# A Hymba layer on one core: sample-step work moved to later attention tiles, and the first instructions of three stages moved ahead of the stage boundaries

## The chip, the cores and the metric

One core of one Trainium2 chip runs the whole kernel. The metric is the device time of one execution in microseconds, the median of three runs. TensorE's clock has two levels here, 1.2 and 2.4 GHz; the profile shows the granted clock as a share of the higher one.

## The reference

The kernel computes one layer of a hybrid decoder for 4096 prompt positions (and 16 meta tokens ahead of them) and for 8 x 8 sample-step tokens:

```python
z = rmsnorm(x, norm_w) @ w_in            # 1024 -> q 512 | k 128 | v 128 | g_attn 512 | u 512 | g_ssm 512
q, k = rope(rmsnorm(q)), rope(rmsnorm(k))
o = sink_softmax(q k / 8, window of 128, sinks) v       # 8 query heads, 2 kv heads
y, state = complex diagonal scan of u in 32 groups of 16 channels, 64 states each
a = rmsnorm(o * silu(g_attn), attn_out_norm_w)
g = gelu(y);  s = g * sigmoid(g @ w_glu + b_glu)
s = rmsnorm(s * silu(g_ssm), ssm_out_norm_w)
out = x + concat(a, s) @ w_out
```

The sample-step tokens attend to a cache of 128 keys and start from given states. Keys, values and states of both kinds of tokens are outputs too. Everything is float32; each product is made as three products of high and low parts (fp32r).

## The kernel before, in words

Four stages follow one another. Each is a block of five instruction streams (SP, POOL, PE, ACT, DVE), and between two blocks all five engines meet at a barrier. So nothing of a later stage starts before the last instruction, and the last awaited transfer, of the earlier one.

**Attention** (`attention_tiles`, names `b_`, PSUM `ps_b`) goes over NT = 33 tiles of 128 tokens. In a tile TensorE projects q, k, v and the gate, transposes keys (L1032, once per tile) and gates (L1038), makes the scores (L949) and the product with the values (L1016). The vector engine (DVE) masks the scores, splits the probabilities into high and low (`split_probs`, L1349), normalizes q and k (`norm_qk`, ends with `b_RK`), and multiplies the output by the gate (`gate_attn`, `b_AT`, L1387). POOL makes the low part of x (`b_XL`, L870), ACT the high part, copies and exponentials. The 64 sample-step tokens are a part of tile 0's projection, and their attention is done in pieces: `samples(t)` does one piece in tile t, at the tiles in `QK_AT, SCORES_AT, MAX_AT, ...`: 7 is the row maximum (DVE), 8 the exponentials (ACT), 9 the normalization (DVE), 10 to 15 the products, gate and norm. DVE's pieces stand between the rotation and `split_probs`; ACT's right after the tile's exponentials. The weights and x of the next stage are loaded, scaled and split here as well (`shared.load`, `shared.high` on ACT, `shared.low` on DVE, L391; `next_high_x` on ACT, `next_low_x` on POOL).

**Early projections** (`early_projections`, `e_`, `ps_e`) make u and the state-space gate in ST = 9 steps s of 464 tokens, each NB = 8 blocks m of 24 matmuls (L559 to L561): u for m = 0 to 3, the gate for m = 4 to 7. A block writes one of seven PSUM banks, and waits for the DVE to have emptied the block seven before (`z_out`). The last bank holds the sums of squares of x, by two matmuls with ones (`total(s)`, L546), from which DVE computes the norm (`rsqrt`, L88 to L94). In a step DVE does `u_out(s,0)`, a part of the state-space parameters (`discretize`), `u_out(s,1)`, `u_out(s,2)`, `discretize`, `u_out(s,3)`, then the gate blocks (`gate_in` L603, `gate_out` L608). SP stores u (L449) and the gate (L454, 36 transfers) to scratch, and at the end the second half of the parameters (`scr_par`, L177).

**State space** (`state_space`, `g_`, `ps_g`) goes over 32 groups. POOL makes tables (`phasors`), DVE small products (`vectors`, names `g_WB`, `g_CB`, `g_CP`), TensorE the group's matrices (L1612 to L1619) and its chunks (L1632); DVE turns inputs and scans. PARs (parameters) and U are loaded by SP from scratch.

**Late projections** (`late_projections`, `l_`, `ps_l`) in NJ = 9 blocks j of 512 tokens: `glu(j)` (48 matmuls, L2051 to L2053) on gelu's high and low parts (`l_GH` ACT, `l_GL` DVE), then per tile the output projection of the attention half (`attention_part(t,h)`, 12 matmuls, L2066 to L2068) and of the state half. SP loads A (attention output), Y, X and the gate in the order in which the code stands.

The order of the work around each boundary is that of the code, written out by hand; no planner moves anything.

Of the kernel before, what the change touches and what calls it, by code (L numbers as in the profile page):

```python
# [12 lines left out]
P = 128  # L13
# [17 lines left out]
T = 16  # L31
# [305 lines left out]
class Shared:  # L337
# [4 lines left out]
    def __init__(self, ctx, nc):  # L342
# [9 lines left out]
        self.XT = sb("XT", [P, KD, SW])  # L352
# [41 lines left out]

def early_projections(nc, I, scr, shared, RAO, USA):

# [4 lines left out]
    with ExitStack() as ctx:  # L401
# [8 lines left out]
        XH, XL = ([X0[hl], sb(f"X{hl}1", [P, KD, SW], F32R)] for hl in "HL")  # L410
# [24 lines left out]
        with nc.Block() as block:  # L435
            @block.sync
            def _(sp):
# [35 lines left out]
                par.store(sp, scr, 1)  # L473
# [8 lines left out]
            def _(act):  # L482
# [18 lines left out]
                for k in range(shared.STAGED, KD):  # L501
                    shared.high(act, k)
# [14 lines left out]
            def _(pool):  # L517
# [56 lines left out]
            def _(dve):  # L574
# [36 lines left out]
                for k in range(shared.STAGED, KD):  # L611
# [24 lines left out]
                for s in range(ST):  # L636
# [8 lines left out]
                    u_out(s, 3)  # L645
                    gate_in(s, 0)
# [21 lines left out]
def attention_tiles(nc, I, O, scr, shared):  # L668


    with ExitStack() as ctx:
# [93 lines left out]
        QK_AT, SCORES_AT, MAX_AT, EXP_AT, NORM_AT, CACHED_AT, NEW_AT, GATE_AT, VALUES_AT, SQUARE_AT, TOTAL_AT = 4, (5, 6), 7, 8, 9, 10, 11, 12, 13, 14, 15  # L765
# [9 lines left out]
        with nc.Block() as block:  # L775
            @block.sync
            def _(sp):
# [73 lines left out]
                for k in range(shared.STAGED, KD):  # L851
                    shared.load(sp, I, k)
                sp.wait_ge(gated, last)
                sp.dma_start(scr["a"][last * P:(last + 1) * P, :], AT[last % 2][:].rearrange("p c q -> p (c q)")).then_inc(a_st[last % 2], 16)
                sp.wait_ge(tail, 64)
# [5 lines left out]
            def _(pool):  # L861
# [43 lines left out]
                for p in range(3):  # L905
# [171 lines left out]
            def _(act):  # L1077
# [137 lines left out]
                for t in range(NT):  # L1215
                    if t >= 2:
                        square_a(t - 1)
                    if t == NT - 1:
# [3 lines left out]
                        shared.high(act, 1)  # L1222
                    if t:
                        exps(t)
                        samples(t)
# [19 lines left out]
                next_high_x(1)  # L1245
                shared.high(act, 2)
                shared.high(act, 3)
                next_high_x(2)
                shared.high(act, 4)
                next_high_x(3)  # L1250
# [4 lines left out]
            def _(dve):  # L1255
# [95 lines left out]
                def samples(t):  # L1351
# [8 lines left out]
                    elif t == MAX_AT:  # L1360
# [15 lines left out]
                    elif t == VALUES_AT:  # L1376
# [920 lines left out]
```

## Time and profile before

| what | value |
|---|---|
| time, median of 3 runs | 1875.1 us (1874.62 to 1875.12) |
| time of the profiled execution | 1875.93 us |
| its span, first to last instruction | 1874.1 us |
| TensorE busy | 1759.9 us, 94% |
| DVE, ACT, POOL busy | 72%, 36%, 28% |
| mean granted TensorE clock | 0.970 |

The times inside the profile are microseconds from the first instruction. 1.8 us of the execution lie around the span. Attention runs to about 750 us, the early projections to 1147, state space to 1388, late projections to the end. A matmul's row gives its start and its duration; matmuls overlap, so their durations do not add up to the time that they take.

### The profile page before, as it was taken

How to read it: one execution, taken by the hardware profiler on the slowest of the kernel's cores; microseconds unless marked ns; L12 is line 12 of the kernel's file. 1: busy time of each engine (PE TensorE's matmuls, PEld its weight loads, DVE VectorE, ACT ScalarE, POOL GpSimd, SP SyncE). 2: the span in 40 equal slices, each digit the busy share in tenths (PEclk: the TensorE clock that was granted, in tenths of full speed). 3: DMA queues.
4: the chain of work that ended last, by engine and by line, in shares of the span. 5: the costliest groups of instructions: out<-in, count | busy, mean ns of one | idle time of the engine just before them, and what ended most of it. 6: DMA issues, size and time to landing. Idle time of an engine off the chain costs nothing. (4 is left out here: it accounts for less than half of the span.)

```text
span 1874.1 us, 26223 instructions
## 1 busy us (share of the span) xinstructions
PE 1759.9 (94%) x8822; PEld 1428.2 (76%) x8822; DVE 1341.9 (72%) x2969; ACT 666.1 (36%) x1668; POOL 527.0 (28%) x618
## 2 busy tenths in 40 slices
PE   6899899999999996899999995999978999999999
PEld 4777677778777774788888883777756888888886
DVE  5787878687887887688989954898827545665632
ACT  5454444445445545332133201354424222222210
POOL 1122112121221222422223304899912101112110
PEclk8999999999999997899999997999988999999999
DMA  6211112142122101333143124566565553554331
GB/s 251 82 60 66 54 60 89 36 142 101 60 73 76 37 25 54 81 96 130 55 123 132 52 82 127 134 174 158 141 132 129 129 142 124 146 124 122 110 115 65
DMA packets 198406, 191.62 MB, mean 102 GB/s; under 512 B 121345, under 2 KB 157185, under 8 KB 198273
## 3 DMA queue, kind: packets, MB, share of 16 engines
q1 hardware_dynamic: 189056, 181.56, 32.9%
q10 hardware_dynamic: 9216, 8.39, 2.2%
q8 instruction: 71, 1.16, 0.3%
q14 instruction: 63, 0.51, 0.1%
HBM read 130.81 MB, written 59.10 MB: 101 GB/s over the span
## 5 line engine op out<-in xcount | busy, mean ns | idle before, releaser
L916 PE MATMUL ps_b<-b_WH,b_XH 128*128 128x512 f32 (+1 forms) x792 | 293.5, 371 | 17.5 <-DVE b_WL L1259 10.6
L917 PE MATMUL ps_b<-b_WL,b_XH 128*128 128x512 f32 (+1 forms) x792 | 283.6, 358 | 0.0
L918 PE MATMUL ps_b<-b_WH,b_XL 128*128 128x512 f32 (+1 forms) x792 | 283.6, 358 | 0.0
L916 PEld LDWEIGHTS ps_b<-b_WH,b_XH 128*128 128x128 f32 x792 | 151.7, 192 | 47.4 <-issue 26.0
L870 POOL TENSOR_TENSOR b_XL<-b_XT,b_XH 128x1024 fp32r<-128x1024 f32 x33 | 79.7, 2416 | 374.3 <-ACT b_XH L1088 324.4
L918 PEld LDWEIGHTS ps_b<-b_WH,b_XL 128*128 128x128 f32 x792 | 151.5, 191 | 22.2
L917 PEld LDWEIGHTS ps_b<-b_WL,b_XH 128*128 128x128 f32 x792 | 152.2, 192 | 19.2
L1154 ACT ACTIVATE b_SM<-ps_b,b_small 128x128 f32<-128x128 f32 x256 | 113.7, 454 | 109.9 <-DVE b_small L1330 107.3
L559 PE MATMUL ps_e<-w_X0H,w_nextH 128*128 128x464 f32 x320 | 123.7, 386 | 2.5 <-POOL e_ONES L518 2.5
L2066 PE MATMUL ps_l<-W_OUTH,l_AH 128*128 128x512 f32 (+1 forms) x264 | 106.7, 404 | 17.8 <-POOL l_AL L2015 13.1
L561 PE MATMUL ps_e<-w_X0H,w_nextL 128*128 128x464 f32 x320 | 121.2, 379 | 0.0
L2166 DVE SCALAR_TENSOR_TENSOR l_OUT<-ps_l,l_small,l_OUT 128x512 f32<-128x512 f32 (+1 forms) x66 | 48.8, 749 | 100.8 <-PE ps_l L2068 100.8
L560 PE MATMUL ps_e<-w_X0L,w_nextH 128*128 128x464 f32 x320 | 121.0, 378 | 0.0
L2015 POOL TENSOR_TENSOR l_AL<-l_A,l_AH 128x512 fp32r<-128x512 f32 (+1 forms) x33 | 42.4, 1286 | 237.9 <-ACT l_AH L1962 237.9
L2067 PE MATMUL ps_l<-W_OUTL,l_AH 128*128 128x512 f32 (+1 forms) x264 | 105.2, 398 | 0.0
L2068 PE MATMUL ps_l<-W_OUTH,l_AL 128*128 128x512 f32 (+1 forms) x264 | 105.0, 398 | 0.0
L2066 PE MATMUL ps_l<-W_OUTH,l_SH 128*128 128x512 f32 (+1 forms) x264 | 102.9, 390 | 0.0
L2068 PE MATMUL ps_l<-W_OUTH,l_SL 128*128 128x512 f32 (+1 forms) x264 | 102.8, 389 | 0.0
L2067 PE MATMUL ps_l<-W_OUTL,l_SH 128*128 128x512 f32 (+1 forms) x264 | 102.7, 389 | 0.0
L1962 ACT ACTIVATE l_AH<-l_A 128x512 fp32r<-128x512 f32 (+1 forms) x33 | 20.5, 622 | 228.9 <-DMA l_A<-scr_a 228.9
L498 ACT ACTIVATE e_TH<-e_TG 128x464 f32<-128x464 f32 x36 | 20.8, 592 | 224.8 <-DVE e_TG L603 224.8
L2158 DVE SCALAR_TENSOR_TENSOR l_OUT<-ps_l,RAO,l_X 128x512 f32<-128x512 f32 (+1 forms) x66 | 48.4, 748 | 72.8 <-DMA out_out<-l_OUT 51.3
(324 smaller groups left out, 4366.0 us busy)
## 6 DMA issues: line engine op xcount, KB each, us to landing
b_XT<-in_xb SPq DMA_DIRECT2D x33, 512.0 KB, 4.0
b_XR<-in_x SPq DMA_DIRECT2D x33, 512.0 KB, 4.7
w_XT<-in_xt SPq DMA_DIRECT2D x36, 464.0 KB, 3.6
l_X<-in_xr SPq DMA_DIRECT2D x32, 512.0 KB, 4.6
out_out<-l_OUT SPq DMA_DIRECT2D x32, 512.0 KB, 3.0
scr_gs<-e_TG SPq DMA_DIRECT2D x36, 232.0 KB, 2.0
scr_u<-w_ST SPq DMA_DIRECT2D x12, 696.0 KB, 3.8
g_U<-scr_u SPq DMA_DIRECT2D x192, 43.5 KB
```

What stands on the lines that cost most here:

```text
L559: pe.matmul(bank(s, m), high, XH[s % 2][:, k, :], start=(k == 0), stop=False)
L560: pe.matmul(bank(s, m), high, XL[s % 2][:, k, :], start=False, stop=False)
L561: mm = pe.matmul(bank(s, m), low, XH[s % 2][:, k, :], start=False, stop=(k == KD - 1))
L870: pool.tensor_tensor(XL[b][:], XT[b][:], XH[b][:].bitcast(F32), ALU.subtract).then_inc(x_lo, 1)
L916: pe.matmul(bank[:, 0:c1 - c0], XH[b][:, k, :], WH[:, k, c0:c1], start=(k == 0), stop=False)
L917: pe.matmul(bank[:, 0:c1 - c0], XH[b][:, k, :], WL[:, k, c0:c1], start=False, stop=False)
L918: mm = pe.matmul(bank[:, 0:c1 - c0], XL[b][:, k, :], WH[:, k, c0:c1], start=False, stop=(k == KD - 1))
L1154: exped.mark(act.activation(SM[:, h, :], scores_of(g)[:, j, t % 2, :], ACT.Exp, bias=NM[:, h:h + 1], scale=RQX[:, h:h + 1], accum_out=SUM[ ...
L2066: pe.matmul(bank, lh, w[0], start=first, stop=False)
L2067: pe.matmul(bank, lh, w[1], start=False, stop=False)
L2068: return pe.matmul(bank, ll, w[0], start=False, stop=last)
L2166: dve.scalar_tensor_tensor(out=o, in0=ps[0:n, 3 + 2 * h, :], scalar=RSS[0:n, i:i + 1], in1=o, op0=ALU.mult, op1=ALU.add).then_inc(o_out, 1)
```

## The change

**Attention.** The sample pieces from the maximum on move one or two tiles later. On ACT the pieces stand behind `values(t + 1)` instead of right behind the tile's exponentials. The maximum and the normalization on DVE become `sample_softmax(t)`, behind `gate_attn(t)`. At the end of the stage DVE makes two instead of three `shared.low` ahead of the last `gate_attn`, and does one more piece of the next x in POOL's place; ACT's and SP's work for the weight rows 1, 4 and 7 moves later.

**Early projections.** The wait for the ones and `total(0)` stand behind block 2 of step 0 instead of behind block 0. In the last step, SP, POOL and DVE do what was the start of state space: five parameter loads, `SWAP`, the store of the parameters ahead of the last gate stores, u of groups 0 and 1, the tables of groups 0 to 3, the vectors of groups 0 to 2. The class `Groups` holds the buffers of that, in room that x of the steps before has left.

**State space to late projections.** The class `Ahead` holds the attention outputs A of the tiles 0 and 1, which are loaded and split within state space. Four of the last eight stores of `scr_ys` go to ACT's queue, and SP no longer waits for 17 stores at the end of state space, but ahead of the last load of Y. In the late projections SP's first loads are X(0) and Y(0), TensorE does both parts of tiles 0 and 1 ahead of `glu(0)`, and DVE adds the attention of tile 0 ahead of `low_g(0)`.

```diff
-        QK_AT, SCORES_AT, MAX_AT, EXP_AT, NORM_AT, CACHED_AT, NEW_AT, GATE_AT, VALUES_AT, SQUARE_AT, TOTAL_AT = 4, (5, 6), 7, 8, 9, 10, 11, 12, 13, 14, 15
+        QK_AT, SCORES_AT, MAX_AT, EXP_AT, NORM_AT, CACHED_AT, NEW_AT, GATE_AT, VALUES_AT, SQUARE_AT, TOTAL_AT = 4, (5, 6), 8, 9, 10, 12, 13, 14, 15, 16, 17
...
                     if t:
                         exps(t)
-                        samples(t)
                     if t + 1 < NT:
                         copy_q(t + 1)
...
                         values(t + 1)
+                    samples(t)
                     if t + 2 < NT:
                         high_x(t + 2)
...
                     if t == NT - 1:
-                        for k in range(3):
+                        for k in range(2):
                             shared.low(dve, k)
                     if t + 1 < NT:
                         norm_qk(t + 1)
                         gate_of(t + 1)
                     if t:
                         gate_attn(t)
+                    sample_softmax(t)
...
+                    if s == ST - 1:
+                        sp.wait_ge(x_acc, 7 * ST)
+                        for t in range(groups.RP - 1):
+                            groups.load_params(sp, t)
+                        sp.wait_ge(z_full, NB * (ST - 1))
+                        sp.dma_start(groups.SWAP[:], I["swap"]).then_inc(groups.const_ld, 16)
                     for m in range(4):
                         if s + 2 < ST:
                             load_x(s + 2, m)
                         store_u(s, m)
+                    if s == ST - 1:
+                        par.store(sp, scr, 1)
+                        sp.wait_ge(u_st[0], 16 * ST // 3)
+                        for t in range(2):
+                            groups.load_u(sp, t)
                     for m in range(4):
                         store_g(s, m)
...
-                par.store(sp, scr, 1)
                 sp.wait_ge(par.stored, 32)
...
+                pool.wait_ge(z_full, NB * (ST - 1))
+                for t in range(4):
+                    groups.phasors(pool, t)
...
-                pe.wait_ge(ones_set, 1)
                 for s in range(ST):
                     for m in range(NB):
                         project(s, m)
-                        if s == 0 and m == 0:
+                        if s == 0 and m == 2:
+                            pe.wait_ge(ones_set, 1)
                             total(0)
...
                     u_out(s, 3)
+                    if s == ST - 1:
+                        for t in range(3):
+                            groups.vectors(dve, t)
...
-                load_params(0)
-                load_params(1)
-                for dst, src in ((SWAP, I["swap"]), (NO, I["out_norm"])):
-                    sp.dma_start(dst[:], src).then_inc(const_ld, 16)
-                for t in range(2, RP - 1):
-                    load_params(t)
-                load_u(0)
-                load_u(1)
-                load_u(2)
+                sp.dma_start(NO[:], I["out_norm"]).then_inc(const_ld, 16)
+                groups.load_u(sp, 2)
...
+                    if t in (20, 21):
+                        ahead.load(sp, t - 20, P, t - 19)
...
-                sp.wait_ge(out_st, 16 * 17)
...
+                    if t in (28, 29):
+                        ahead.low(pool, t - 28, P)
...
+                    if t in (24, 25):
+                        ahead.high(act, t - 24, P)
+                y_out.wait(act, tile(G - 1))
+                for i in range(4, 8):
+                    act.dma_start(scr["ys"][256:512, 8 * i:8 * i + 8].rearrange("(g h) b -> h g b", h=SG), YSS[SG * i:SG * i + SG, 16:32, :]).then_inc(out_st, 16)
...
-                load_a(0)
+                load_x(0)
                 load_y(0)
-                load_x(0)
-                load_a(1)
...
-                for h in range(2):
-                    attention_part(0, h)
+                for t in range(2):
+                    for h in range(2):
+                        attention_part(t, h)
                 glu(0)
-                for h in range(2):
-                    attention_part(1, h)
...
+                add_attention(0)
                 low_g(0)
-                add_attention(0)
                 steps(0)
```

On DVE, the sample maximum (`b_s_small`) stands in tile 7 between the end of the rotation (`b_RQK`) and the split of the probabilities (`b_PC`, `b_PP`):

```order
L1289 TENSOR_TENSOR b_RQK<-b_RQK,b_ZS 128x128
L1362 TENSOR_REDUCE b_s_small<-w_ST 128x4
L1364 TENSOR_TENSOR b_s_small<-b_s_small 128x4
L1366 TENSOR_TENSOR b_s_small<-b_s_small 128x4
L1367 TENSOR_SCALAR b_s_small<-b_s_small 128x4
L1349 TENSOR_TENSOR b_PC<-ps_b,b_HALF 128x512
L1349 TENSOR_TENSOR b_PP<-ps_b,b_HALF 128x512
```

In the changed kernel it stands on the same engine in tile 8, at the tile's end, between the gated output (`b_AT`) and the mask on the next tile's scores:

```order
L1416 TENSOR_TENSOR b_RK<-b_RQK,b_small 128x128
L1425 SCALAR_TENSOR_TENSOR b_GATE<-b_TH,ps_b 128x512
L1504 TENSOR_TENSOR b_AT<-ps_b,b_GT 128x512
L1483 TENSOR_REDUCE b_s_small<-w_ST 128x4
L1485 TENSOR_TENSOR b_s_small<-b_s_small 128x4
L1487 TENSOR_TENSOR b_s_small<-b_s_small 128x4
L1488 TENSOR_SCALAR b_s_small<-b_s_small 128x4
L1438 COPY_PREDICATED ps_b<-b_TAKE,ps_b 128x4x128
```

The four instructions have left the place ahead of `b_PC`, and stand behind `b_RK` and `b_AT`. On SP's queue, the boundary from the early projections (the last gate stores `scr_gs`, the parameter store `scr_par`) to state space (the two branches are the barrier) reads before:

```order
L449 DMA scr_u<-w_ST 128x1392 x4
L454 DMA scr_gs<-e_TG_10301 128x464
L454 DMA scr_gs<-e_TG_10302 128x464
L454 DMA scr_gs<-e_TG_10301 128x464
L454 DMA scr_gs<-e_TG_10302 128x464
L177 DMA scr_par<-params 128x16x198
L435 UNCONDITIONAL_BRANCH
L1491 UNCONDITIONAL_BRANCH
L1500 DMA g_PAR<-scr_par 128x198 x2
L1534 DMA g_SWAP<-in_swap 128x384
L1534 DMA g_NO<-in_out_norm 128x8
L1500 DMA g_PAR<-scr_par 128x198 x3
```

and in the changed kernel, at the same place:

```order
L548 DMA scr_u<-w_ST 128x1392 x4
L177 DMA scr_par<-params 128x16x198
L454 DMA g_U_10300<-scr_u 128x1x87 x6
L454 DMA g_U_10301<-scr_u 128x1x87 x6
L553 DMA scr_gs<-e_TG_10325 128x464
L553 DMA scr_gs<-e_TG_10326 128x464
L553 DMA scr_gs<-e_TG_10325 128x464
L553 DMA scr_gs<-e_TG_10326 128x464
L534 UNCONDITIONAL_BRANCH
L1635 UNCONDITIONAL_BRANCH
L1656 DMA g_NO<-in_out_norm 128x8
L454 DMA g_U_10302<-scr_u 128x1x87 x6
```

The parameter store and two groups of `g_U` have come ahead of the last four gate stores, and `g_PAR` and `g_SWAP` ahead of all that is shown; behind the barrier only `g_NO` and the third group's u are left ahead of the weights.

## Rows read from the trace of the kernel before

**Rows 1.** Windows: busy us (instructions) per engine, then granted clock, DMA share, GB/s

```profile
804.40:1088.00 283.60, 282.52 (x1328) 248.73 (x1327) 252.63 (x568) 75.34 (x94) 70.00 (x49) 1.00 0.30 94
1088.00:1135.30 47.30, 47.29 (x225) 41.77 (x223) 17.16 (x25) 2.96 (x5) 0.00 (x0) 1.00 0.23 91
1168.00:1380.10 212.10, 209.07 (x1040) 163.63 (x1040) 173.72 (x236) 93.86 (x316) 178.12 (x250) 0.98 0.59 146
1445.30:1874.00 428.70, 424.58 (x1906) 349.71 (x1906) 220.77 (x337) 89.53 (x142) 65.08 (x51) 0.99 0.43 121
```

**Rows 2.** Timeline of PE, key transposes: tiles 7 to 9, and twelve tiles later on

```profile
184.99 0.27 PE L1032 MATMUL ps_b<-b_ID,b_RK 128*128 128x128 f32 x1
...
208.24 0.33 PE L1032 MATMUL ps_b<-b_ID,b_RK 128*128 128x128 f32 x1 [1.12 <-DVE b_RK L1301]
...
233.24 0.33 PE L1032 MATMUL ps_b<-b_ID,b_RK 128*128 128x128 f32 x1 [1.12 <-DVE b_RK L1301]
...
258.57 0.33 PE L1032 MATMUL ps_b<-b_ID,b_RK 128*128 128x128 f32 x1 [1.12 <-DVE b_RK L1301]
...
372.71 0.27 PE L1032 MATMUL ps_b<-b_ID,b_RK 128*128 128x128 f32 x1
...
620.51 0.27 PE L1032 MATMUL ps_b<-b_ID,b_RK 128*128 128x128 f32 x1
```

**Rows 3.** Timeline of DVE: a sample piece in tile 7, and a steady tile

```profile
199.38 2.27 DVE L1364 TENSOR_TENSOR b_s_small<-b_s_small 128x4 f32<-128x4 f32 x1
...
603.10 0.70 DVE L1323 COPY_PREDICATED ps_b<-b_TAKE,ps_b 128x512 f32<-128x512 int32 x1 [2.22 <-PE ps_b L949]
```

**Rows 4.** Timelines of PE and DVE at the end of attention

```profile
739.46 1.92 PE L1016 MATMUL ps_b<-b_PP,b_VS 128*64 128x512 f32 x4
...
743.05 0.68 DVE L1387 TENSOR_TENSOR b_AT<-ps_b,b_GT 128x512 f32<-128x512 f32 x1
...
750.99 0.76 PE L559 MATMUL ps_e<-w_X0H,w_nextH 128*128 128x464 f32 x1 [2.49 <-POOL e_ONES L518]
```

**Rows 5.** Timelines of PE and DVE, step 0 of the early projections

```profile
764.46 1.14 PE L546 MATMUL ps_e<-e_ACC,e_ONES 128*128 128x464 f32 x1 [5.41 <-POOL e_ACC L532]
...
766.48 0.64 DVE L88 TENSOR_SCALAR e_VX<-ps_e 128x464 f32<-128x464 f32 x1 [10.80 <-PE ps_e L546]
...
794.28 1.00 DVE L595 TENSOR_TENSOR w_ST<-ps_e,e_RXB 128x400 f32<-128x400 f32 x1
...
804.37 0.38 PE L559 MATMUL ps_e<-e_XH,w_nextH 128*128 128x464 f32 x1
```

**Rows 6.** Windows, the stretch at the half clock behind a short wait of PE in the late projections

```profile
1422.50:1425.90 3.40, 3.40 (x9) 2.40 (x8) 1.61 (x2) 0.42 (x1) 0.00 (x0) 0.52 1.00 180
```

**Rows 7.** Timelines and waits of SP and PE, early projections to state space; last, the DMA issues

```profile
1137.65 0.46 SPq L177 DMA_DIRECT2D scr_par<-params  x1
SPq L435 <- DMA scr_par<-params: 6.2, 1, 6.2
1147.26 0.80 SPq L1500 DMA_DIRECT2D g_PAR<-scr_par  x2
1151.91 1.01 PE L1612 MATMUL ps_g<-g_CP,g_PAR 128*16 128x256 f32 x2 [16.63 <-DVE g_CP L1778]
1161.25 1.13 PE L1632 MATMUL ps_g<-g_U,g_W 128*128 128x265 f32 x4 [1.19 <-DMA g_U<-scr_u]
scr_gs<-e_TG SPq DMA_DIRECT2D x36, 232.0 KB, 2.0
```

**Rows 8.** Timelines and waits of SP and PE, state space to late projections

```profile
1381.30 3.91 SPq L1523 DMA_DIRECT2D scr_ys<-g_YSS  x8
SPq L1560 <- DMA out_states<-g_XS: 1.3, 1, 1.3
1388.72 5.75 SPq L1898 DMA_DIRECT2D l_Y<-scr_y  x4
1421.28 0.47 PE L2051 MATMUL ps_l<-l_GH,W_GLUH 128*128 128x512 f32 x1 [2.59 <-DVE l_GL L2114]
```

More of the change, by code:

```diff
@@ L351, in __init__ @@
         self.X0 = {hl: self.at("X", KD * SW * "HL".index(hl), "w_X0" + hl, [P, KD, SW], F32R) for hl in "HL"}
-        self.XT = sb("XT", [P, KD, SW])
+        self.XT = high.enter_context(nc.sbuf_tensor("w_XT", [P, KD, SW], F32, side="right"))
         self.ST = sb("ST", [P, 9 * (QK + P)])
@@ L398, in early_projections @@
+def early_projections(nc, I, scr, shared, groups, RAO, USA):
     NB, NPC = 8, 4
@@ L500, in _ @@
                 act.sem_inc(x_hi, NPC)
-                for k in range(shared.STAGED, KD):
+                for k in range(4, KD):
                     shared.high(act, k)
@@ L610, in _ @@
                 dve.sem_inc(x_lo, NPC)
-                for k in range(shared.STAGED, KD):
+                for k in range(3, KD):
                     shared.low(dve, k)
@@ L850, in _ @@
                 sp.dma_start(O["v_win"], VS[last % 3][:]).then_inc(tail, 16)
-                for k in range(shared.STAGED, KD):
-                    shared.load(sp, I, k)
+                shared.load(sp, I, 5)
+                shared.load(sp, I, 6)
                 sp.wait_ge(gated, last)
                 sp.dma_start(scr["a"][last * P:(last + 1) * P, :], AT[last % 2][:].rearrange("p c q -> p (c q)")).then_inc(a_st[last % 2], 16)
+                shared.load(sp, I, 7)
                 sp.wait_ge(tail, 64)
@@ L904, in _ @@
                         tables(t + 2)
-                for p in range(3):
+                for p in range(2):
                     next_low_x(p)
@@ L1245, in _ @@
                 next_high_x(1)
+                shared.high(act, 1)
                 shared.high(act, 2)
+                next_high_x(2)
+                next_high_x(3)
                 shared.high(act, 3)
-                next_high_x(2)
-                shared.high(act, 4)
-                next_high_x(3)
                 square_a(NT - 1)
@@ L1473, in tile @@
+        out_st = ahead.rest_st
         def tile(t):
@@ L1800, in scan @@
                     z_steps.link(dve, T_, dve.tensor_tensor(CZ[t % RM][:, :, 0:n], bcast_mid(ZS[:], 2), CS[t % RC][:, :, 0:n], ALU.mult))
-                for t in range(3):
-                    vectors(t)
                 turn_inputs(0)
                 turn_inputs(1)
-                vectors(3)
+                groups.vectors(dve, 3)
                 scan(0)
@@ L1836, in late_projections @@
         X = [sb(f"X{i}", [P, D]) for i in range(3)]
-        A = [sb(f"A{i}", [P, 4, P]) for i in range(2)]
-        AH, AL = ([sb(f"A{hl}{i}", [P, 4, P], F32R) for i in range(2)] for hl in "HL")
+        AH, AL = ahead.AH, ahead.AL
         OUT = [sb(f"OUT{i}", [P, D]) for i in range(2)]
@@ L1845, in late_projections @@
         y_ld, gs_ld = [sem(f"y_ld{i}") for i in range(2)], sem("gs_ld")
-        x_ld, a_ld = [sem(f"x_ld{i}") for i in range(3)], [sem(f"a_ld{i}") for i in range(2)]
+        x_ld = [sem(f"x_ld{i}") for i in range(3)]
         g_hi, g_lo = sem("g_high"), sem("g_low")
-        a_hi, a_lo = sem("a_high"), sem("a_low")
+        a_lo = ahead.lo
         z_full, z_th = sem("z_full"), sem("z_tanh")
@@ L1913, in load_a @@
                 def load_a(t):
[L1914 to L1917 removed]
+                    sp.wait_ge(a_lo, t - 1)
+                    ahead.load(sp, t, rows(t)[1], block_of(t))
                 def store(t):
@@ L1957, in high_a @@
                 def high_a(t):
-                    act.wait_ge(a_ld[t % 2], 16 * (t // 2 + 1))
-                    if t >= 2:
-                        act.wait_ge(a_full, 2 * (t - 1))
-                    n = rows(t)[1]
-                    act.activation(AH[t % 2][:, :, 0:n], A[t % 2][:, :, 0:n], ACT.Copy).then_inc(a_hi, 1)
+                    act.wait_ge(a_full, 2 * (t - 1))
+                    ahead.high(act, t, rows(t)[1])
                 def tanh(j, m):
@@ L2036, in _ @@
                         if t + 2 < NT:
-                            low_a(t + 2)
+                            ahead.low(pool, t + 2, rows(t + 2)[1])
             @block.tensor
```

253 lines of the change are left out of this document (146 added, 107 removed).

## The prediction

> **What bounds the kernel now.** I read the granted clock and the span first, then the windows by stage, then TensorE's waits, then timelines around each. Inside the stages TensorE is the bound: it is busy for 282.52 of 283.60 us in steps 1 to 7 of the early projections, 209.07 of 212.10 us in state space, 424.58 of 428.70 us in the late projections behind 1445.3 [rows 1]. So an edit inside these stretches gains nothing by itself, and a microsecond saved ahead of them is kept to the end. What is left are five places where TensorE stands. One is attention's tiles 7 to 9: the key transposes are 23.25, 25.00 and 25.33 us apart, 73.58 together, while later ones are (620.51 - 372.71)/12 = 20.65 us apart [rows 2]; three of these are 61.95, an excess of 11.6 us. The others are the end of attention (7.9 us from the last gated output to the next stage's first matmul, 2.49 of them the last wait [rows 4]), step 0 of the early projections (5.41 [rows 5]), the start of state space (16.63 and 1.19 [rows 7]) and the start of the late projections (2.59 [rows 8] and what is ahead of it). At each restart the clock is at its lower level for a while; behind the wait of 2.59 us it was granted 0.52 over 3.40 us [rows 6], which is 1.6 us of lost work.
>
> **The change part by part.**
>
> *Tiles 7 to 9: 9.4 us.* The sample maximum, exponentials and normalization are in these tiles, and they stand ahead of the work that feeds TensorE: DVE's ahead of the split probabilities, ACT's ahead of its copies. Behind `gate_attn` DVE has an idle stretch of 2.22 us in a steady tile, until scores come [rows 3]. The two DVE pieces move into that idle stretch. Their bulk before was one instruction on 128x4 elements that took 2.27 us [rows 3]; without such a stall the pieces are under 2 us each, so the idle stretch covers them. If that cover were gone they would cost what they cost now, 2.6 and 4.7 us (the periods less 20.65). ACT's exponentials move behind `values(t + 1)`; now they delay ACT's high part of x for tile t + 2, and so POOL's low part, which then falls on DVE's normalization. I leave 2.2 us for that, the stall of 2.27 seen once. 11.6 - 2.2 = 9.4. Both ends: 6 (a stall in each of the three tiles, 11.6 - 3 x 2.0) and 11.6 (nothing left). The later pieces (six, each moved by one or two tiles) cost nothing new, their TensorE work is the same.
>
> *End of attention and step 0: 5.5 us.* The last `b_AT` starts at 743.05, but its matmuls end at 739.46 + 1.92 = 741.4 [rows 4]; DVE was making the third `shared.low`. With two, `b_AT` starts at about 741.4 to 741.8. From there to the first matmul of the early projections is 750.99 - 743.05 = 7.9 us (POOL's sums, norm, store, barrier), which follows along; the ones (2.49 us wait, mostly barrier) are no longer waited for there. First matmul at about 749.0, 2.0 earlier. Then block 0 takes 764.46 - 5.41 - 750.99 = 8.06 us (half clock), and `total(0)` stood 5.41 us behind it. Now blocks 1 and 2 stand between: a warm block of 24 matmuls is 283.60/1328 x 24 = 5.1 us [rows 1]. `total(0)` is at 749.0 + 8.06 + 10.2 = 767.2; the sums that it needs were ready at 764.4 and come no later, so it does not wait. DVE reads them about 1 us later, at 768.2. Now something is late next: DVE's chain from there (norm, the low parts of x, `u_out(0,0)`, `discretize`, `u_out(0,1)`) took from 766.48 to 795.3 [rows 5], 28.8 us, and ends at 797.0. Block 0 of step 1 needs the bank that `u_out(0,1)` empties. TensorE gets there at 767.6 + 5 x 5.1 + 0.4 = 793.4 and waits for 3.6 us; queued behind are all its later blocks, and nobody but DVE's later outputs waits for these. It restarts at 797.0 against 804.37 [rows 5], 7.4 us earlier, and pays 1.6 to 1.9 us of half clock like [rows 6]: 5.5. Ends: 3 (a slower DVE chain beside POOL) and 10.9 (no wait: 2.0, the 5.41, and 3.5 us of half clock behind it).
>
> *Early projections to state space: 8.1 us.* Before, the parameters are stored at 1137.65, SP waits 6.2 us for their landing, and the first instruction of state space is at 1147.26, 2.9 us behind that; TensorE starts at 1151.91 [rows 7]. Now the parameter store is ahead of the gate stores and lands under them; the last thing awaited is the last gate store, issued right ahead of 1137.65 with 2.0 us to landing [rows 7], so 1139.7, and state space begins at 1142.6. Parameters, tables and vectors are there; what TensorE's stream still waits for is `g_NO`, issued first behind the barrier: 0.4 us of issue and a landing like the 2.0 of [rows 7]. It starts at 1145.0, 6.9 earlier; the u of group 1 is loaded too, so the 1.19 us wait goes. What is moved into step 8 counts there: on SP five parameter loads, `SWAP`, the store and 12 loads of u ahead of the gate stores; on POOL 32 table instructions; on DVE nine, of which three take less than the 4.7 us from 1147.26 to 1151.91. What hides them is step 8's TensorE work, 47.29 of 47.30 us, beside which DVE is busy for 17.16 us and POOL for nothing [rows 1]: 30 us are free on DVE for at most 14. Without that cover the last gate store comes late: 19 issues of 0.43 us (0.46 for the store, 0.80 for two loads [rows 7]) are 8.2 us on SP, and up to 3 of them could remain at the end. Ends: 5 and 9.
>
> The Trainium skill ("DMA: Bandwidth & Descriptors", Latency and other measured facts) gives a fixed cost of about 2 us to each DMA, however small. By it the load of `g_NO` behind the barrier keeps a wait of that size, and the term cannot reach the 9.3 us that no wait at all would give (1142.6 against 1151.91). The trace agrees (2.0 us [rows 7]).
>
> *State space to late projections: 2.1 us.* SP issues four stores fewer, 4 x 3.91/8 = 1.95, and does not wait 1.3 us for the last [rows 8]: the stage begins 3.3 earlier. A(0) needs no load, so TensorE works at once on the attention parts and the wait for `l_AL` as such goes; but the end is set by Y(0), gelu and `l_GL`. Y(0) is issued behind X(0)'s 512 KB instead of A(0)'s 256 KB; at 5.75 us for four Y of 256 KB that is 0.4 to 1.4, I take 0.8. `glu(1)` (1421.28 [rows 8]) comes 2.5 earlier. Since attention(1) no longer fills the time ahead of it, TensorE's 2.59 us wait grows to about 8, and the half clock behind it lasts longer; 0.4 for that. Ends 0 and 4.
>
> Sum 9.4 + 5.5 + 8.1 + 2.1 = 25.1. The profiled execution is 1875.93 us, 0.8 above the median 1875.1 of the runs shown: 1850.8, and on the median's scale 1850.0.
>
> **The rivals.** A change under 0.2%, 3.75 us, is about what cannot be told from none.
>
> - *No new wait in step 1* (chance 0.13). If DVE's chain is 4 us shorter beside an emptier POOL, +3.6 + 1.6; with nothing left of the excess in tiles 7 to 9, +2.2: a gain of 32.5, 1842.6. For it: DVE's chain there runs beside POOL, and two engines that hold each other up could fall otherwise. Against: POOL's work there is the same, and stands at the same place of the chain.
> - *The stalls move with the pieces* (0.10). The 2.27 us on 128x4 elements [rows 3] is DVE held up by something. Nine tiles hold moved pieces; at four more stalls, 9.1 lost, 1859. The Trainium skill ("SBUF — State Buffer", Who interferes with whom) names the cause: DVE and GpSimd share a port pair that one instruction locks as a whole. By it a piece moved beside POOL's low part of x stalls anew. The row agrees with a stall of that kind.
> - *The boundaries give less* (0.20). The chains behind them are not shortened as I think: 7 from the tiles, 3 at step 0, 4 and 0 at the boundaries, 14: 1861.
> - *Nothing in sum* (0.04): the place where TensorE waited is only given back by DVE later, at every one of the five: 1872 to 1878.
> - *DVE becomes the bound of the early projections* (0.03), the other side. The wait of 3.6 us at step 1 comes again in each of the seven steps behind it, 7 x (3.6 + 1.6) = 36.4, more than 25.1: 1886. It decides from 3.6 us per step without catching up. Against: DVE is busy for 252.63 of 283.60 us [rows 1], so 3.9 us per step are free, and it catches up in one.
>
> **How the numbers follow.** The forecast itself has 0.50, with 1846 to 1855. The range 1843 to 1862 takes in the smaller gains and all but the end of the larger, and leaves out about 2 in 10. Faster 0.93, same 0.04, slower 0.03.
>
> **What would show it.** In the profile after: key transposes 21 to 23 us apart all through tiles 7 to 10; the last `b_AT` at its matmuls' end; no wait at `total(0)`, one of 3 to 4 us on `u_out(0,1)` at step 1; the first matmul of state space 7 us earlier against step 8's end, waiting for `g_NO`; PE's first late matmul right behind the barrier, then a wait of about 8 us ahead of `glu(1)`. The prediction is wrong if step 8 has waits of TensorE, if tiles 8 to 17 show new long periods, or if the new wait at step 1 is absent or repeats.

## The result

| | us | ratio to the kernel before, 95% interval |
|---|---|---|
| before, median (6 runs) | 1875.11 | |
| changed, median (6 runs) | 1866.87 (1862.54 to 1868.80) | 0.9949 (0.9927 to 0.9971) |
| changed, second set (8 runs, beside 11 of before at 1876.22) | 1865.89 | 0.9956 (0.9943 to 0.9969) |

The change makes the kernel 8 to 10 us faster. The forecast was 25 us, 1850, with a range from 1843 to 1862, so the time is outside. The page of the changed kernel shows first what went otherwise: its span is 8.5 us shorter, but TensorE is busy for 1770.8 us instead of 1759.9, with the same 8822 matmuls.

```profile
span 1865.6 us, 26223 instructions
PE 1770.8 (95%) x8822; PEld 1429.5 (77%) x8822; DVE 1336.1 (72%) x2970; ACT 666.1 (36%) x1668; POOL 521.7 (28%) x617
```

I cut both timelines of TensorE at the same instructions. A stretch goes from one marker's start to the next one's.

| stretch of TensorE | before | after | difference | forecast |
|---|---|---|---|---|
| 3rd to 18th key transpose (tiles 7 to 9 in it) | 334.3 | 325.3 | -9.0 | -9.4 |
| last key transpose to first early matmul | 27.6 | 25.0 | -2.6 | -2.0 |
| first early matmul to last | 383.9 | 384.5 | +0.6 | -3.5 |
| last early matmul to first state-space matmul | 17.0 | 8.45 | -8.6 | -6.9 |
| from there to the first L1648 (L1747 after) | 16.0 | 13.8 | -2.3 | -1.2 |
| state space behind that | 211.75 | 210.6 | -1.1 | 0 |
| last state-space matmul to the last stall | 65.7 | 65.6 | -0.1 | -2.1 |
| from the last stall to the last matmul's start | 424.2 | 435.4 | +11.2 | 0 |

The rows add up to -11.9 us, the starts of the last matmuls differ by -8.5. The other 3.4 us are outside the rows. 2.6 are in the first three tiles, ahead of anything changed (82.58 us to the third key transpose, 79.97 before); this varies by as much between executions of one kernel (82.58 and 79.47 in two of the changed one). 0.8 are between the 18th and the last key transpose (309.1 and 309.85 us), and these belong to the change: the last sample piece has moved from tile 15 to tile 17, and the period behind the 18th transpose is 21.4 us instead of 20.8. So the sample pieces' 9.0 us are 8.2 in net.

In the changed kernel the waits of TensorE are these (engine and line that waits, who releases, us in all, times, longest), which answer to the ones in [rows 4, 5, 7, 8]:

```profile
PE ps_e L658 <- POOL e_ACC L641: 9.1, 3, 5.3
PE ps_g L1711 <- DMA g_NO<-in_out_norm: 8.1, 1, 8.1
PE ps_l L2120 <- DVE l_GL L2182: 8.0, 2, 7.8
PE ps_l L2135 <- PEq L135: 5.8, 1, 5.8
```

The wait for `g_CP` of 16.63 us has become one for `g_NO` of 8.07, and that for `l_AL` one for the barrier alone, with 7.8 us ahead of `glu(1)`. All that was named. The sums `e_ACC` cost 9.1 us in three waits, the longest of 5.3, where there was one of 5.41 [rows 5] and a short one.

**Attention.** The key transposes of the three tiles [rows 2] and around (timeline of TensorE):

```profile
187.38 0.27 PE L1148 MATMUL ps_b<-b_ID,b_RK 128*128 128x128 f32 x1
207.88 0.27 PE L1148 MATMUL ps_b<-b_ID,b_RK 128*128 128x128 f32 x1
228.58 0.33 PE L1148 MATMUL ps_b<-b_ID,b_RK 128*128 128x128 f32 x1
250.58 0.33 PE L1148 MATMUL ps_b<-b_ID,b_RK 128*128 128x128 f32 x1 [1.04 <-DVE b_RK L1416]
273.01 0.27 PE L1148 MATMUL ps_b<-b_ID,b_RK 128*128 128x128 f32 x1
```

The periods are 20.5, 20.7, 22.0 and 22.4 us. What is left is in the tile of the exponentials (22.0), as forecast, and in the one behind it (22.4), where TensorE waits for nothing, but has a granted clock of 0.72 in the 4.42 us behind the 1.04 us wait at 250.58 (window, columns as in [rows 1]):

```profile
250.58:255.00 4.42, 3.99 (x21) 3.02 (x21) 1.26 (x2) 1.39 (x3) 1.36 (x3) 0.72 0.44 137
```

In the tile of the exponentials DVE's first step of the normalization started inside POOL's low part of x (timelines of DVE and POOL), and took 1.87 us where the same instruction took 0.23 one tile before; the maximum's step on 128x4 elements, 2.27 us in [rows 3], takes 0.16 in its new place:

```profile
225.64 0.23 DVE L88 TENSOR_SCALAR b_small<-b_small,w_EPSX 128x10 f32<-128x10 f32 x1
...
230.74 0.16 DVE L1485 TENSOR_TENSOR b_s_small<-b_s_small 128x4 f32<-128x4 f32 x1
...
245.02 2.40 POOL L986 TENSOR_TENSOR b_XL<-b_XT,b_XH 128x1024 fp32r<-128x1024 f32 x1 [12.31 <-ACT b_XH L1204]
...
245.58 1.87 DVE L88 TENSOR_SCALAR b_small<-b_small,w_EPSX 128x10 f32<-128x10 f32 x1
```

DVE is free when POOL ends: 245.02 + 2.40 = 247.42, and 245.58 + 1.87 = 247.45. By the lock of the port pair that the Trainium skill describes ("SBUF — State Buffer", Who interferes with whom) the step should end just behind POOL's. These rows agree.

**Step 0 of the early projections** (timeline of TensorE; the sums, and the first matmul of step 1; compare [rows 5]):

```profile
760.15 0.94 PE L658 MATMUL ps_e<-e_ACC,e_ONES 128*128 128x464 f32 x2
781.60 1.92 PE L658 MATMUL ps_e<-e_ACC,e_ONES 128*128 128x464 f32 x2 [5.35 <-POOL e_ACC L641]
827.48 1.04 PE L658 MATMUL ps_e<-e_ACC,e_ONES 128*128 128x464 f32 x2 [2.78 <-POOL e_ACC L641]
```

`total(0)` does not wait any more, but `total(1)` waits for 5.35 us, with a granted clock of 0.50 in the 3.4 us behind it, and `total(2)` for 2.78. The wait that the prediction put on the bank of block 0 of step 1 is not there: `u_out(0,1)` ends at 789.85 and TensorE comes to that block only at 794.21.

**Late projections.** Windows of 380 us each, behind the last stall, before and after (columns as in [rows 1]: the stretch, its length, then each engine's busy time with its number of instructions, then the granted clock):

```profile
1460.00:1840.00 380.00, 380.00 (x1723) 316.19 (x1722) 205.13 (x307) 84.26 (x136) 63.05 (x49) 1.00 0.46 128
```

```profile
1460.00:1840.00 380.00, 380.00 (x1677) 310.21 (x1676) 199.07 (x299) 83.42 (x135) 60.66 (x48) 0.99 0.44 120
```

TensorE never waits in either, the clock is at its upper level in both, and it does 1723 matmuls in the one and 1677 in the other. A matmul takes 220.5 and 226.6 ns of the window on average. These means hold some 100 narrow matmuls of 2 and 64 columns. From start to start, two 128x512 matmuls are 226 or 227 ns apart in the kernel before, and 228 to 241 in the changed one, but for 4% and 1% of them. Nothing in the diff touches this stretch's instructions. What the diff does move is where its buffers lie: `Ahead` is allocated ahead of them, with 1024 and 1152 bytes per partition of state-space outputs. So in the changed kernel all the buffers of the late projections, among them the split A, gelu and S, start at 160 modulo 256 bytes, while before they started at 32. The weights W_GLU and W_OUT start at 32 in both. Every late matmul takes one operand from either group: A and S are stationary against W_OUT, which moves, and gelu moves against W_GLU, which is stationary (the expectations below call all of the first group stationary, which is wrong for gelu). I call A, gelu and S the data operands.

### The profile page after: what moved, and what is told of

The parts are those of the page before. It is cut to its first block and busy times, and to the rows that moved or that the text cites. A ratio compares the mean times of both kernels' runs of the same rounds, so it can differ in the third digit from the quotient of the medians.

```text
span 1865.6 us, 26223 instructions
## 1 busy us (share of the span) xinstructions
PE 1770.8 (95%) x8822; PEld 1429.5 (77%) x8822; DVE 1336.1 (72%) x2970; ACT 666.1 (36%) x1668; POOL 521.7 (28%) x617
## 5 line engine op out<-in xcount | busy, mean ns | idle before, releaser
L1032 PE MATMUL ps_b<-b_WH,b_XH 128*128 128x512 f32 (+1 forms) x792 | 293.5, 371 | 18.1 <-DVE b_WL L1374 11.5
L2135 PE MATMUL ps_l<-W_OUTH,l_AH 128*128 128x512 f32 (+1 forms) x264 | 107.7, 408 | 10.3 <-PEq L135 5.8
L1568 ACT ACTIVATE l_AH<-l_A 128x512 fp32r<-128x512 f32 (+1 forms) x33 | 20.5, 622 | 225.0 <-DMA l_A<-scr_a 224.5
L607 ACT ACTIVATE e_TH<-e_TG 128x464 f32<-128x464 f32 x36 | 20.8, 593 | 222.4 <-DVE e_TG L715 222.4
```

Of the source, the lines that this page charges most:

```text
L1032: pe.matmul(bank[:, 0:c1 - c0], XH[b][:, k, :], WH[:, k, c0:c1], start=(k == 0), stop=False)
L2135: pe.matmul(bank, lh, w[0], start=first, stop=False)
```

## The experiments

The stretches of the table are used throughout. "Last stretch" is from the last stall to the last matmul's start. A single profile is behind each of them, and medians are of the runs named.

### Does the rate belong to the kernel, and to the layout?

Four kernels. Two are the kernels as they are. The third:

```diff
         self.YSS, self.XS = (ctx.enter_context(nc.sbuf_tensor("l_" + n, [P, G, k], F32)) for n, k in (("YSS", 8), ("XS", 9)))
+        ctx.enter_context(nc.sbuf_tensor("l_PAD", [P, 96], F32))
         self.A, self.AH, self.AL = sb("A"), sb("AH", F32R), sb("AL", F32R)
```

and the fourth, in the late projections of the kernel before:

```diff
+        sb("PAD", [P, 32])
         Y = [sb(f"Y{i}", [P, 4, T, 32]) for i in range(2)]
```

Expected of the kernel before:

> The kernel before, unchanged, profiled once more, to see whether the rate of TensorE in the late projections is a property of the kernel. In its first profile the stretch behind the last stall (from 1445.35) took 428.7 us to the end; in the changed kernel the same 1856 matmul rows took 439.9 us at the same granted clock. Theory L (layout: the rate hangs on where the buffers of the late projections lie in SBUF): 428.5 to 429 us again. Theory R (the rate differs from execution to execution or from chip to chip): any value from 428 to 441.

Of the changed kernel:

> The changed kernel, unchanged, profiled and timed on the same chip. Theory L: 439 to 440.5 us from the last stall to the end again, and 8 us faster than before. Theory R: another value, by several us.

Of the changed kernel with 384 bytes:

> The changed kernel with 384 unused bytes per partition between the state-space outputs and the buffers of the late projections. All operands that the late matmuls take as stationary (the split A, gelu and S) lie 128 bytes off the phase that they had before, modulo 512, while the weights W_GLU and W_OUT lie where they lay; the 384 bytes bring the old phase back (modulo 512 bytes), though not the old addresses. Theory L in the form 'phase': the last stretch takes 429 us, the kernel is 11 us faster than the changed one, about 1856. Theory L in the form 'place' (which region): still 440. Theory R: no relation.

Of the kernel before with 128 bytes:

> The kernel before, with 128 unused bytes per partition ahead of the buffers of its late projections and nothing else changed. Theory L 'phase': the last stretch goes from 428.7 to 440 us and the kernel is 11 us slower, 1886. Theory 'place' and theory R: within 1 us of the kernel before.

| kernel | data operands at, weights at (mod 256) | last stretch | median us | ratio to before |
|---|---|---|---|---|
| before, again | 32, 32 | 423.6 | 1872.63 (1 run) | |
| changed, again | 160, 32 | 435.5 | 1865.89 (8) | 0.9956 (0.9943 to 0.9969) |
| changed + 384 bytes | 32, 32 | 424.1 | 1856.48 (4) | 0.9900 (0.9876 to 0.9925) |
| before + 128 bytes | 160, 32 | 436.4 | 1889.91 (4) | 1.0080 (1.0048 to 1.0111) |

The rate is a property of the kernel and comes again. 384 unused bytes make the changed kernel 9 us faster, and 128 unused bytes make the kernel before slower by 12 us in the last stretch and by 14 in the median (10 or 11 were expected; its four runs go from 1882.6 to 1894.0). The window of 380 us, in the changed kernel with 384 bytes and then in the kernel before with 128:

```profile
1460.00:1840.00 380.00, 380.00 (x1721) 314.88 (x1721) 201.94 (x303) 83.38 (x135) 61.12 (x48) 1.00 0.43 121
```

```profile
1460.00:1840.00 380.00, 380.00 (x1670) 310.38 (x1669) 201.15 (x302) 83.64 (x135) 61.65 (x48) 0.99 0.45 124
```

1721 and 1670 matmuls in the same time, with no instruction different from its parent.

### Which phase?

The 384 bytes bring back the phase (the start modulo a power of two) modulo 512 as well as 256, and the data operands' own phase as well as the one relative to the weights. The same line with 24, 32 and 48 instead of 96 elements tells apart the first two; with the weights moved too the last two:

```diff
-        ctx.enter_context(nc.sbuf_tensor("l_PAD", [P, 96], F32))
+        ctx.enter_context(nc.sbuf_tensor("l_PAD", [P, 32], F32))
...
+        ctx.enter_context(nc.sbuf_tensor("W_PAD", [P, 56], F32))
         w3 = [parts(ctx, *shape) for shape in (("W_GLU", 4, DS), ("W_OUT", KD, D))]
```

This one has all at 0; the one with the weights at 160 has 64 and 32 elements in the two places.

Of 96 bytes:

> The changed kernel with 96 unused bytes in the place of the 384: the stationary operands of the late matmuls lie at 0 modulo 512 bytes (the weights stay at 288). With 288 the last stretch took 424.1 us to the last matmul's start, with 416 (the changed kernel) 435.4. If the cost comes from a stationary row's 512 bytes straddling a 512-byte line, and only then less or more, 0 should be at least as fast as 288: 424 or less. If what counts is the phase relative to the weights, 0 is slow like 416: 435.

Of 128 bytes:

> The same with 128 unused bytes: the stationary operands at 32 modulo 512, which is the weights' phase modulo 256, but not modulo 512. If the phase counts modulo 256: 424 us for the last stretch; modulo 512: 435 or something between.

Of all at 0:

> The changed kernel with 128 bytes unused as in the run at 32, and 224 more ahead of the weights W_GLU and W_OUT, so that weights and stationary operands of the late matmuls all lie at 0 modulo 256. So far the last stretch took 424 to 425 us with both at 32, 435.4 with the stationary ones at 160 and 438.5 with them at 0 (weights at 32). Relative theory (what counts is that the two operands have one phase modulo 256): 424 to 425. Absolute theory (the stationary operand must lie at 32, or not at 0 or 160): 436 to 439.

Of the weights at 160:

> The changed kernel with the weights of the late matmuls at 160 modulo 256 and the stationary operands at 32, where they were fast. Relative theory: 435 us for the last stretch, like the changed kernel, whose difference is the same 128. Absolute theory: 424 to 425.

Of the data operands at 96:

> The changed kernel with the stationary operands at 96 modulo 256, the weights at 32. Both theories: between 425 and 439, as no run has that phase; if the cost were a matter of 64-byte phases (32 against 0), 96 and 160 would be alike, and 160 is slow: 435.

| data operands at, weights at (mod 256) | difference | last stretch | median us |
|---|---|---|---|
| 32, 32 (not the same modulo 512) | 0 | 425.1 | 1854.30 (2 runs) |
| 0, 0 | 0 | 425.2 | 1851.54 (2) |
| 32, 160 | 128 | 435.5 | 1867.84 (4) |
| 96, 32 | 64 | 438.6 | 1868.32 (4) |
| 0, 32 | -32 | 438.5 | 1865.27 (3) |

Every kernel of the two tables with a difference of 0 modulo 256 has 423.6 to 425.2 us, and every one with another has 435.4 to 438.6. The absolute theory (that the data operands must lie at 32) falls twice: all at 0 is fast, and data operands at 32 with the weights at 160 are slow. So does the form modulo 512. The window of the weights at 160:

```profile
1460.00:1840.00 380.00, 380.00 (x1677) 310.21 (x1676) 198.83 (x299) 83.08 (x135) 60.45 (x47) 0.99 0.43 120
```

The padding moves every buffer of the late projections, and so those of DVE, ACT and POOL too. The traces tell these apart. In the changed kernel, 128x512 matmuls on W_OUT with no instruction of DVE, ACT or POOL within 0.2 us are 232.3 ns apart (276 of them between 1460 and 1790 us), and those with one all the time 232.6 (518); in the kernel before it is 226.7 and 227.2. So the slow rate does not come from the other engines' accesses. DMA transfers were not told apart in this way; their share of the window is alike, 0.46 and 0.44. Nor does it hang on which operand moves: in `glu`, where the weights are stationary, a difference of 0 gives 226.7 ns, of 128 232.9 to 233.3, and of 64 and -32 233.3 to 233.4; on W_OUT it is 226.7, 232.5 and 233.3.

The early projections show the phase too, but it evens out there. The moving operand's rows lie 1856 bytes apart, which is 64 modulo 256, and both the weights and the first x buffer start at 32. In the even steps from 2 on of the kernel before, the mean time from the start of the product with the low part of x to the next start is 210, 207, 214 and 210 ns for the first four of the eight rows of x, and 210, 206, 213 and 209 for the other four. In the changed kernel the second x buffer starts at 224, 192 further, and in the odd steps the same values stand one row later (210, 210, 206, 213, then 209, 211, 205, 213). Each block goes through all four phases twice, so the means of all three products are alike: 210.6 ns in these steps of both kernels, and 211.3 in the odd steps of the kernel before, where the buffer starts at 128 and no row has the weights' phase. That is 0.5 us over the stage, which agrees with the stretches of the next table (330.0 from step 1 on with `total(0)` back, 330.4 to 330.5 before). The attention projections have both operands at 32 in both kernels, and are 227 to 229 ns apart in both.

What stays open is the mechanism. In the late projections a difference of 0 is the fastest and 64 among the slowest, in the early ones' rows 64 is the fastest; no run here tells why.

### The place of total(0) and total(1)

Both on the changed kernel with 384 bytes. The first puts the sum back behind block 0, the second moves the next one:

```diff
-                        if s == 0 and m == 2:
+                        if s == 0 and m == 0:
                             pe.wait_ge(ones_set, 1)
                             total(0)
```

```diff
-                        if m == 5 and s + 1 < ST:
+                        if m == (7 if s == 0 else 5) and s + 1 < ST:
                             total(s + 1)
```

Of the first:

> The changed kernel with the 384 bytes, and the first sum of squares (and the wait for the ones) back behind block 0 of step 0. My prediction held that moving it saves 5.5 us less what the end of attention gives. New theory T: the gain is eaten by the next sum, total(1), which waits for DVE's low parts and ACT's squares of step 1's x; both hang on the first sum. T expects that TensorE's time from the first matmul to step 1's first is 52 to 54 us again (51.5 to 52.1 with the move), and the kernel at most 2 us slower than with the 384 bytes alone (1856.5). The prediction's theory expects 5 us or more.

Of the second:

> The changed kernel with the 384 bytes, and total(1) behind block 7 of step 0 instead of behind block 5. T: TensorE comes to total(1) 10 us later, when its sums (781.3 in that kernel) are ready, so the wait of 5.35 us and the half clock behind it go; what is late next is the bank for block 0 of step 1, which u_out(0,1) empties at 789.9 - the wait that the prediction named, of 2 to 3 us. Step 1's first matmul comes 3 to 5 us earlier (from 794.1 to 789.5 to 791), and of this 1 to 4 us are left at the end of step 8, since the norm of step 1 comes later. Rival: the norm of step 1 then delays the low parts of x, the squares and total(2), and nothing is left.

| | first matmul to step 1's | step 1's first to the last | together | median us |
|---|---|---|---|---|
| before (3 profiles) | 51.9 to 53.4 | 330.4 to 330.5 | 382.3 to 383.9 | |
| changed + 384 bytes | 52.1 | 333.0 | 385.1 | 1856.48 |
| total(0) back | 53.5 | 330.0 | 383.5 | 1853.72 (4 runs) |
| total(1) last | 47.2 | 339.7 | 386.9 | 1855.27 (4) |

Putting `total(0)` back costs 1.4 us in step 0 and gives 3.0 behind it: the move is worth nothing, and rather costs 1.6 us (0.8 to 1.6 over all profiles: 384.3 to 385.1 in nine with the move, 383.5 in two with it back). T, the theory of the expectation, named the place and the sign of step 0, but not that the steps behind lose what is won. Moving `total(1)` makes step 0 another 5 us shorter, as T said, and loses 7 in the steps behind: the rival was right. The wait on the bank of block 0 of step 1, which the prediction named for the change as it stands, is in this kernel (2.87 us at 786.2). The wait for the sums went on to `total(2)`, from 2.57 to 6.88 us (timeline of TensorE, that kernel):

```profile
782.39 0.94 PE L658 MATMUL ps_e<-e_ACC,e_ONES 128*128 128x464 f32 x2
823.68 1.91 PE L658 MATMUL ps_e<-e_ACC,e_ONES 128*128 128x464 f32 x2 [6.88 <-POOL e_ACC L641]
```

Each sum hangs on the one before: sum, norm and low parts of x on DVE, squares on ACT, additions on POOL, next sum. An earlier TensorE only meets that chain sooner. And the move starts the chain later: `total(0)` runs 17.8 us behind the first early matmul, and 14.9 with it back.

### Y(0) or X(0) first?

On the changed kernel with 128 bytes:

```diff
-                load_x(0)
                 load_y(0)
+                load_x(0)
```

> The changed kernel with 128 unused bytes (stationary operands at 32), and the two first loads of the late projections in the other order: Y(0), then X(0). My prediction counted 0.8 us of loss for X(0) being ahead, 2.1 us of gain for the whole boundary; the two traces show that the boundary's stretch, from the last matmul of state space to the last stall, did not get shorter by more than about 1 us (65.7 to 65.1, 63.8 in one run). Theory Y: X's 512 KB ahead hold Y back; with Y first gelu starts 1 to 2 us earlier, and glu(0), glu(1) and the last stall with it: 62 to 63 us. Rival: Y's landing is set by its own small packets, and X behind it only delays the attention add: no change, 64 to 65 us.

Neither held. The stretch to the last stall got longer, 68.2 us against 63.6 in its parent and 61.9 to 65.6 in all kernels with X first, and the median is 1860.70 (4 runs) against 1854.30 (2). Y comes earlier, but the second tile's attention part needs the bank that DVE empties by adding X(0), and `glu(0)` is queued behind it on TensorE (timelines of TensorE and DVE, that kernel):

```profile
1378.99 0.77 PE L2136 MATMUL ps_l<-W_OUTH,l_AH 128*128 128x512 f32 x1 [3.93 <-DVE l_OUT L2227]
```

```profile
1378.09 1.41 DVE L2227 SCALAR_TENSOR_TENSOR l_OUT<-ps_l,RAO,l_X 128x512 f32<-128x512 f32 x2 [20.48 <-DMA l_X<-in_xr]
```

So X first is part of what makes two attention parts ahead of `glu(0)` possible, and its price of 0.8 us in the prediction is not a price that another order saves.

### The sum, without the layout

The sample pieces alone, on the kernel before (positions, ACT's place, `sample_softmax` on DVE, as in the change's diff), and the changed kernel with 128 bytes and `total(0)` back.

> The kernel before with the sample pieces of attention moved as in the change, and nothing else. From the traces: the stretch from the third to the eighteenth key transpose took 332.7 to 334.3 us in kernels without the move, 323.9 to 325.7 with it (327.3 once). Prediction's term: 9.4 us. Both the prediction and the stretches say 8.5 to 9.5 us faster than before, and no change in the late projections (424 us for the last stretch), whose layout is the old one. Rival (part of the gain came from another edit of the change): under 6 us.

> The changed kernel with 128 unused bytes ahead of the late buffers (stationary operands and weights at one phase modulo 256) and total(0) back behind block 0. By the stretches: attention -8.9 and -2.5, the early projections' 0.4 less than with the move (about -0.8 against before), start of state space -10.9, late boundary -1: 23 us, so 1852 to 1853, against 1876 for the kernel before. If total(0)'s place is worth nothing either way, 1854 to 1856 as with the phase alone.

| kernel | 3rd to 18th transpose | last stretch | median us | ratio to before |
|---|---|---|---|---|
| sample pieces alone | 324.0 | 424.2 | 1867.85 (8 runs) | 0.9956 (0.9941 to 0.9971) |
| changed, 128 bytes, total(0) back | 325.7 | 424.1 | 1854.75 (4) | 0.9889 (0.9870 to 0.9908) |

The sample pieces alone give 7.7 us in the medians (1875.52 beside them) and 8.7 to 10.3 in the stretch, less 0.7 behind it. That is as much as the whole change as it stands. The mended kernel is 20.8 us faster than the kernel before and about 11 faster than the changed one; it misses the 1852 to 1853 of the stretches by 2 us and is inside the 1854 to 1856 that were expected if the place of `total(0)` is worth nothing. The place of `total(0)` does not show in the medians: 1854.75 with it back against 1854.30 and 1856.48 with it moved.

## Why the prediction was wrong, point by point

- *"So an edit inside these stretches gains nothing by itself, and a microsecond saved ahead of them is kept to the end."* This step failed. I took the late projections' 424.58 of 428.70 us [rows 1] as fixed, and so put the change's effect on them at nothing, since it leaves their instructions alone. It moves their buffers by 128 bytes modulo 256 against the weights, and that costs 11.2 us (shown by adding the effect to the kernel before and by taking it from the changed one). None of the rivals had it. Without it the change would have been at 1854 to 1856, inside the range.
- *Tiles 7 to 9, 9.4 us.* Right: 9.0, with the one stall that was expected, at the place that was expected, and 7.7 us for this part by itself. *"The later pieces [...] cost nothing new"* was off by the 0.8 us behind the 18th transpose.
- *"the sums that it needs were ready at 764.4 and come no later, so it does not wait"* was right, and so was DVE's chain of 28.8 us (28.6 from 761.21 to 789.85). *"TensorE gets there at 767.6 + 5 x 5.1 + 0.4 = 793.4"* failed: it counts `total(1)` as 0.4 us and does not ask when its sums are there. They are late by 5.35 us, and a half clock follows. The sum itself puts `total(0)` 2.8 us behind the readiness of its sums (767.2 against 764.4), and charges nothing of that to `total(1)`. The term of 5.5 us, of which 2.0 were the end of attention (measured 2.6), was -0.6 + 2.6 = 2.0.
- *Early projections to state space, 8.1 us.* Right in every step, and too small: 8.6 + 2.3 = 10.9. State space begins 6.8 us behind the last early matmul where I had 7.7, and `g_NO` landed 1.6 us after its issue, where I took 2.4. It is the wait that was named (8.07 us on `g_NO`, 16.63 before [rows 7]). The moved work was hidden in step 8, as said: no wait of TensorE there.
- *State space to late projections, 2.1 us.* 0.1 in the first profile, and 0 to 3.7 and 1.2 on average in the eleven of the kernels with this edit and X first. The late stage began 2.5 us earlier against the end of state space (6.2 us behind its last matmul, 8.7 before) instead of 3.3. Y(0) took 7.36 us to issue behind X(0), not 5.75, and landed 11.5 us after it began, not 9.9: the 0.8 us was 1.6. The wait of about 8 us ahead of `glu(1)` is there, at 7.83.
- Of the 16.6 us between the forecast and the profiled execution, 11.2 are the layout, 3.1 the mis-sized terms of the sum in net (above all step 0, 4.1 us too high), 0.8 the last sample piece, 2.6 the first tiles of that execution, less 1.1 that state space happened to be shorter. The terms as measured give some 21 to 22 us without the layout, and the mended kernel shows 20.8.
- The rivals: *no new wait in step 1* had its condition (no wait on that bank), but with another wait in its place, and no gain. *DVE becomes the bound of the early projections* was the nearest in spirit: the chain through DVE sets the sums' times, but TensorE loses 2.5 us over eight steps and not 5 in each. Its threshold is worked out with eight steps where the window of [rows 1] holds seven: 30.97 us free on DVE are 4.4 per step and not 3.9, which makes the rival a little less likely still.

## What to carry to other kernels

A new buffer moves all that is allocated behind it. Where a stage is bound by matmuls, write down the starts of both operands of the matmuls modulo 256 before and after, and compare the number of matmuls in equal windows of the two traces: the same instructions at the same granted clock should give the same number. When a wait in a chain over several engines is taken away, look at the next instruction that waits for a product of the same chain, not only at the buffer that is freed last; a small edit that is kept by its first stretch can be lost in the next ones, so cut the trace from the edit to the stage's end.

## What the runs showed of the hardware

- 128x512 fp32r matmuls with 128-column stationary operands, back to back, started 226.7 ns apart when both operands' starts in a partition were the same modulo 256 bytes, 232.5 with a difference of 128 bytes and 233.3 with 64 and -32, whichever of the two operands was stationary, and with the other engines idle as well as busy. A window of 380 us held 1723 matmuls of all widths in the kernel before and 1677 in the changed one. The stretch of 1906 matmuls, 1800 of them 128x512, took 423.6 to 425.2 us with a difference of 0 in seven profiles (426.9 to 427.5 in three others, which lost some 3 us to the clock near its end: 0.65 and 0.77 were granted from 1792 to 1810 us in one of them), 435.4 to 436.4 with 128, 438.6 with 64 and 438.5 with -32. The absolute phase (0 or 32) made no difference. The same starts modulo 512 were not needed.
- The matmuls of 464 columns, whose moving rows step through the phases by 64 bytes, showed a pattern of four in the spacing behind the second product (205 to 214 ns by row), which moved by one row with the start of the buffer. It evens out within a block to 0.7 ns.
- Some stretches repeat closely (24.97 to 24.98 us from the last key transpose to the first early matmul in twelve profiles), but state space behind its first products took 208.5 to 215.2 us over sixteen profiles, and the time to the third key transpose was 77.8 to 82.9. The medians of kernels that differ by less than 3 us are not told apart by them; the stretches are.
